# Sparse-attention scores of a two-layer decoder trunk: from one fp32 product to three products of split operands

## What is computed

```
q: (512, 8 heads, 128)   k_cmp, k_slc, k_win: per group of 4 heads
kc = compress(k_cmp)                                # 31 keys of 128
p_c = softmax(q @ kc.T * scale + bias)              # masked
p_s = softmax(q @ k_slc.T * scale + bias)           # causal
p_w = softmax(q @ k_win.T * scale + bias)           # causal
o = g0 * (p_c @ v_cmp) + g1 * (p_s @ v_slc) + g2 * (p_w @ v_win)
h = h + concat(y_mla, o * silu(g_nsa), y_mem) @ w_out
```

## Time and profile before

| | |
|---|---|
| median of 3 runs | 2171.14 us (2170.78 to 2171.8) |
| profiled execution | 2172.06 us |
| its span, first to last instruction | 2170.3 us |
| TensorE busy | 2151.5 us (99%) |
| VectorE busy | 1350.6 us (62%) |
| ScalarE busy | 920.8 us (42%) |
| GpSimd busy | 579.5 us (27%) |
| mean granted TensorE clock | 0.999 |

### The profile page before, as it was taken

One profiled execution on the slowest core, in us unless ns is written; L12 is line 12 of the kernel. 1 busy time (PEld: TensorE's weight loads), 2 busy tenths in 40 slices (PEclk: granted clock), 3 DMA queues, 4 the chain that ended last, 5 costly groups with the idle time before them and its releaser, 6 DMA issues. The chain is left out here.

```text
span 2170.3 us, 32485 instructions
## 1 busy us (share of the span) xinstructions
PE 2151.5 (99%) x12292; PEld 1810.8 (83%) x12292; DVE 1350.6 (62%) x2244; ACT 920.8 (42%) x1558; POOL 579.5 (27%) x771
## 2 busy tenths in 40 slices
PE   9999999999999999999999999999999999999998
PEld 8988888888888878888888899899886778788887
DVE  6632456655542237568649778877776648666876
ACT  6432333333332434434444444444433455555443
POOL 2626122223221002112001444444311255221120
PEclk9999999999999999999999999999999999999999
DMA  8645444444445436648644886878747966554674
GB/s 311 205 140 137 125 130 130 118 128 135 137 123 186 128 99 203 222 148 212 175 156 120 203 202 162 202 185 193 176 152 237 293 216 198 173 193 145 226 164 146
DMA packets 222423, 376.19 MB, mean 173 GB/s; under 512 B 22623, under 2 KB 102191, under 8 KB 220099
## 3 DMA queue, kind: packets, MB, share of 16 engines
q1 hardware_dynamic: 125152, 185.36, 27.8%
q0 software_dynamic: 63152, 126.20, 24.2%
q10 hardware_dynamic: 33971, 62.63, 7.9%
HBM read 310.30 MB, written 63.83 MB: 172 GB/s over the span
## 5 line engine op out<-in xcount | busy, mean ns | idle before, releaser
L283 PE MATMUL PS<-A,wsp 128*128 128x512 f32 (+2 forms) x3156 | 693.8, 379 | 2.9 <-issue 1.7
L283 PEld LDWEIGHTS PS<-A,wsp 128*128 128x128 f32 (+1 forms) x3156 | 564.2, 188 | 119.0 <-issue 9.1
L250 DVE TENSOR_TENSOR wsp<-wraw,wsp 128x1024 fp32r<-128x1024 f32 (+1 forms) x295 | 356.5, 1212 | 468.6 <-ACT wsp L243 467.0
L283 PE MATMUL PS<-wsp,A 128*128 128x512 f32 x2352 | 616.2, 403 | 0.0
L243 ACT ACTIVATE wsp<-wraw 128x1024 fp32r<-128x1024 f32 (+1 forms) x295 | 304.9, 1039 | 509.6 <-PE PS L283 406.7
L283 PEld LDWEIGHTS PS<-wsp,A 128*128 128x128 f32 x2352 | 423.8, 189 | 77.5 <-issue 4.8
L2044 PE MATMUL PS<-A,wsp 128*128 128x512 f32 x640 | 222.6, 397 | 0.0
L2046 PE MATMUL PS<-A,wsp 128*128 128x256 f32 x640 | 166.4, 280 | 0.0
L2001 DVE TENSOR_TENSOR wsp<-wraw,wsp 128x1024 fp32r<-128x1024 f32 x80 | 111.3, 1394 | 39.3 <-ACT wsp L1983 39.1
L2044 PEld LDWEIGHTS PS<-A,wsp 128*128 128x128 f32 x640 | 116.2, 188 | 21.8
L2046 PEld LDWEIGHTS PS<-A,wsp 128*128 128x128 f32 x640 | 120.7, 189 | 6.2
(11 more groups left out here) (455 smaller groups left out, 2841.4 us busy)
## 6 DMA issues: line engine op xcount, KB each, us to landing
wraw<-in_even_w_in_dram SPq DMA_DIRECT2D x112, 512.0 KB, 3.7
wraw<-in_odd_w_in_dram SPq DMA_DIRECT2D x96, 512.0 KB, 4.7
wraw<-in_w_out_dram SPq DMA_DIRECT2D x74, 512.0 KB, 4.6
wraw<-in_mem_w_kv_dram SPq DMA_DIRECT2D x32, 512.0 KB, 4.8
wraw<-in_w_out_dram POOLq DMA_DIRECT2D x24, 512.0 KB, 6.5
yO<-stage ACTq DMA_DIRECT2D x12, 1024.0 KB
yE<-stage ACTq DMA_DIRECT2D x10, 1024.0 KB
wraw<-in_odd_w_in_dram POOLq DMA_DIRECT2D x20, 512.0 KB, 8.8
```

The lines of the kernel that those rows point to most:

```text
L250: nc.vector.tensor_tensor(wsp[:, q, 1, :, 0:j["cols"]], wraw[:, q, :, 0:j["cols"]], wsp[:, q, 0, :, 0:j["cols"]].bitcast(F32), ALU.subtrac ...
L283: mm = nc.tensor.matmul(dst, lhs, rhs, start=(s == 0 and kk == 0 and i == 0), stop=(s == j["spc"] - 1 and kk == 1 and i == 2))
```

## The change

The query and key tiles of the sparse heads are now typed float32r. After a load, ScalarE writes a rounded copy of each into a further tile (`act_nsa_high`), and VectorE replaces the loaded tile by itself less that copy (`dve_nsa_low`). A score is three accumulating products: high query by high keys, low query by high keys, high query by low keys. Keys are loaded and split once for a group of four heads, in a buffer for each group, with the loads of head 0 and of head 4; the other heads load a query and a bias only. The bias now goes ahead of the keys.

The splits of head 0 stand ahead of SEQ1 in both queues: behind the latent attention on ScalarE, behind the fills of P and the gate product on VectorE. Those of head h > 0 stand four steps before its first unit, which is unit k = 8 of head h-1: on ScalarE behind exponential 8 of that head, on VectorE behind normalisation 7. Heads 0 and 4 have three operations on each engine (compressed with selected keys, 544 columns; window keys, 512; query, 512), the others one (query). TensorE waits for the splits (rot_low) ahead of a head's first score.

```diff
+        NSA_AHEAD = 4
         def act_seq(act, t):
...
                 if x < len(t.units):
                     seq_exp(act, t, x)
+                if t.l and x + NSA_AHEAD in t.start[1:8]:
+                    act_nsa_high(act, t.start.index(x + NSA_AHEAD))
...
                 if 0 <= x - 1 < len(t.units):
                     seq_norm(dve, t, x - 1)
+                if t.l and x + NSA_AHEAD in t.start[1:8]:
+                    dve_nsa_low(dve, t.start.index(x + NSA_AHEAD))
...
+        def nsa_operands(h):
+
+            keys = [(nsaKcs[h // 4], nsaKcsH[h // 4]), (nsaKw[h // 4], nsaKwH[h // 4])] if h % 4 == 0 else []
+            return keys + [(nsaQ[h % 2], nsaQh[h % 2])]
+
+        def act_nsa_high(act, h):
+
+            act.wait_ge(a_ld[h % 2], SEQ1.ld0[0] + SEQ1.units[SEQ1.start[h]]["ld"])
+            for whole, high_ in nsa_operands(h):
+                nc.scalar.activation(high_, whole.bitcast(F32), ACT.Copy).then_inc(rot_high, 1)
+
+        def dve_nsa_low(dve, h):
+
+            dve.wait_ge(rot_high, nsa_splits(h))
+            for whole, high_ in nsa_operands(h):
+                nc.vector.tensor_tensor(whole, whole.bitcast(F32), high_.bitcast(F32), ALU.subtract).then_inc(rot_low, 1)
...
+            def products(pe, bank, i, key, o, w):
+
+                if i == ORDER[0] and key == 0 and o <= NPAD:
+                    pe.wait_ge(rot_low, nsa_splits(h))
+                low, high_ = (nsaKcs, nsaKw)[key][grp], (nsaKcsH, nsaKwH)[key][grp]
+                rows = slice(i * P, i * P + P)
+                nc.tensor.matmul(bank[:, 0:w], nsaQh[r][:, rows], high_[:, o:o + w], start=True, stop=False)
+                nc.tensor.matmul(bank[:, 0:w], nsaQ[r][:, rows], high_[:, o:o + w], start=False, stop=False)
+                return nc.tensor.matmul(bank[:, 0:w], nsaQh[r][:, rows], low[:, o:o + w], start=False, stop=True)
...
             def load_qk(pool, s_):
-                pool.dma_start(nsaQ[r], yO[1024 + h * P:1152 + h * P, :]).then_inc(s_, 16)
+                pool.dma_start(nsaQ[r].bitcast(F32), yO[1024 + h * P:1152 + h * P, :]).then_inc(s_, 16)
+                pool.dma_start(nsaB[r], biasD[:, h, :]).then_inc(s_, 16)
+                if h % 4:
+                    return
                 for k in range(2):
-                    pool.dma_start((nsaKs, nsaKw)[k][r], yO[2560 + 256 * k + grp * P:2688 + 256 * k + grp * P, :]).then_inc(s_, 16)
-                pool.dma_start(nsaB[r], biasD[:, h, :]).then_inc(s_, 16)
+                    dst = (nsaKcs[grp][:, NPAD:NPAD + 512], nsaKw[grp])[k]
+                    pool.dma_start(dst.bitcast(F32), yO[2560 + 256 * k + grp * P:2688 + 256 * k + grp * P, :]).then_inc(s_, 16)
...
             act_att(act, MLA)
+            act_nsa_high(act, 0)
             act_seq(act, SEQ1)
...
             dve.wait_ge(p_zero, 5)
+            dve_nsa_low(dve, 0)
             dve_seq(dve, SEQ1)
```

More of the change, by code:

```diff
@@ L3425, in build, with nsa_splits @@
         nsaK0 = A[:, 16:20, :].rearrange("p k t -> p (k t)").bitcast(F32)
-        nsaQ, nsaKw = [[nsaK0[:, o:o + 512], S[:, 8192 + o1:8704 + o1]] for o, o1 in ((0, 0), (1024 + NPAD, 512))]
-        nsaKcs = [nsaK0[:, 512:1024 + NPAD], S[:, 10240:10752 + NPAD]]
-        nsaKc, nsaKs = [[k[:, o:o + n] for k in nsaKcs] for o, n in ((0, NPAD), (NPAD, 512))]
+        nsaQ = [A[:, 16, :], S_rounded[:, 8192:8704]]
+        nsaQh = [A[:, 15, :], A[:, 35, :]]
+        nsaK0r = A[:, 17:20, :].rearrange("p k t -> p (k t)")
+        nsaK0h = A[:, 32:35, :].rearrange("p k t -> p (k t)")
+        nsaKcs = [nsaK0r[:, 0:512 + NPAD], S_rounded[:, 10240:10752 + NPAD]]
+        nsaKcsH = [nsaK0h[:, 0:512 + NPAD], S_rounded[:, 15264:15776 + NPAD]]
+        nsaKw = [nsaK0r[:, 512 + NPAD:1024 + NPAD], S_rounded[:, 8704:9216]]
+        nsaKwH = [nsaK0h[:, 512 + NPAD:1024 + NPAD], S_rounded[:, 15776 + NPAD:16288 + NPAD]]
+        ROT_SPLITS = 9
+        def nsa_splits(h):
+            return ROT_SPLITS + h + 1 + 2 * (1 + (h >= 4))
+        def nsa_operands(h):
[9 more added lines that the diff above has]
+                nc.vector.tensor_tensor(whole, whole.bitcast(F32), high_.bitcast(F32), ALU.subtract).then_inc(rot_low, 1)
         nsaB = [a_tiles(36, 3)[:, 0:LB], S[:, 13312:13312 + LB]]
@@ L3435, in nsa_head @@
             r, grp = h % 2, h // 4
-            keys = (nsaKs[r], nsaKw[r], nsaKc[r])
+            def products(pe, bank, i, key, o, w):
[6 more added lines that the diff above has]
+                return nc.tensor.matmul(bank[:, 0:w], nsaQh[r][:, rows], low[:, o:o + w], start=False, stop=True)
@@ L3438, in score @@
             def score(i, which, w):
-                q = nsaQ[r][:, i * P:i * P + P]
                 if i == 3:
-                    return lambda pe, bank: nc.tensor.matmul(bank[:, 0:w], q, keys[which][:, 0:w], start=True, stop=True)
+                    return lambda pe, bank: products(pe, bank, i, which % 2, NPAD if which == 0 else 0, w)
                 if which == 0:
-                    return lambda pe, bank: nc.tensor.matmul(bank[:, 0:NPAD + w], q, nsaKcs[r][:, 0:NPAD + w], start=True, stop=True)
+                    return lambda pe, bank: products(pe, bank, i, 0, 0, NPAD + w)
@@ L3444, in score @@
                 if which == 1:
-                    return lambda pe, bank: nc.tensor.matmul(bank[:, 0:w], q, nsaKw[r][:, 0:w], start=True, stop=True)
+                    return lambda pe, bank: products(pe, bank, i, 1, 0, w)
                 return None
             def load_qk(pool, s_):
-                pool.dma_start(nsaQ[r], yO[1024 + h * P:1152 + h * P, :]).then_inc(s_, 16)
+                pool.dma_start(nsaQ[r].bitcast(F32), yO[1024 + h * P:1152 + h * P, :]).then_inc(s_, 16)
+                pool.dma_start(nsaB[r], biasD[:, h, :]).then_inc(s_, 16)
@@ L3453, in load_qk @@
                 if h == 0:
                     pool.wait_ge(cmp_out, 32)
-                pool.dma_start(nsaKc[r], cmpD[grp, :, 0:NPAD]).then_inc(s_, 16)
+                pool.dma_start(nsaKcs[grp][:, 0:NPAD].bitcast(F32), cmpD[grp, :, 0:NPAD]).then_inc(s_, 16)
             def load_v(pool, s_):
@@ L3472, in nsa_head @@
                                       gate=gtmS[:, i, col:col + 1], first=which == 0, last=which == 2))
-            return head_units(h, units, ld=80 * (h // 2 + 1), vld=48 * (h // 2 + 1), vn=3, out_gate=nsaG[r],
+            return head_units(h, units, ld=32 * (h // 2 + 1) + (0 if r else 48 * (grp + 1)), vld=48 * (h // 2 + 1), vn=3, out_gate=nsaG[r],
                               gate_rows=yO[5120 + h * P:5248 + h * P, :], load_qk=load_qk, load_v=load_v)
-        SEQ1 = Seq(1, [u for h in range(8) for u in nsa_head(h)] + [u for h in range(4) for u in mem_head(1, h, yO, 3584, 6144, 320, 192)], OUT1A, h1D, 1)
+        SEQ1 = Seq(1, [u for h in range(8) for u in nsa_head(h)] + [u for h in range(4) for u in mem_head(1, h, yO, 3584, 6144, (224, 128)[h % 2], 192)], OUT1A, h1D, 1)
         def pe_nsa_gates(pe):
```

## The result

The changed kernel takes 2177.35 us (median of 15 runs, 2175.75 to 2183.75), the kernel before 2171.09 (15 runs): a ratio of 1.0028, 95% interval 1.0022 to 1.0035. It is 6.3 us slower, where 2171.4 was forecast and 2175.8 was the upper end. A second profile of the same kernel (e11) had the fill at 1831.98. That is +4.6 of the +6.3.

What follows compares the result with a forecast made beforehand. TensorE, busy 2151.5 of 2170.3 us, was taken to bound the kernel; −4.0 products, +3.0 start, +1.1 group 1 keys and +0.2 query splits gave +0.3, so 2171.4 us, range 2167.5 to 2175.8.

Steps and rivals of the forecast that it cites:

- products, eight heads: Scores of the sparse heads: three split products cost 4.17 us a head against 4.67, saving 4.0 us over eight heads.
- start of head 0, the gap: Ahead of head 0's first score: TensorE waits for VectorE's subtractions, score 3.25 us late, net cost +3.0 us (2.7 to 3.4).
- rival 4: The 3.3 us gap ahead of head 0 lowers TensorE's clock to 1.2 GHz, adding 3.0 us: 2174.4 us; chance 0.07.
- keys of group 1, head 3: At k=8 of head 3, three high parts delay unit 6's eviction and transpose 7: +1.1 us (0.5 to 2).
- query splits, the others: One query split for each of heads 1 to 3 and 5 to 7, nearly hidden: +0.2 us in sum (0 to 1).
- rival 2: In all scores, a product costs only its columns, with no floor: 9.0 us saved, 2166.4 us; chance 0.04.
- the dear bound of the products: Sparse-head scores at 0.231 us for 512 columns and 0.12 for narrow products: 0.3 us saved a head, 2.4 in all.
- the 0.2% called undetectable: Whole kernel: a change under 0.2% (4.3 us) is about what measurement cannot tell from none.
- covered by the same stall: Head 3, transpose 8: normalisation 8 ends near 1916.9, transpose runs at 1917.2 after transpose 7's stall, so no further cost.
- free, or a tenth now and then: Query splits, judged in head 1: slack of 0.1 and 0.6 us at transposes 7 and 8, so almost no cost.
- rival 3: Query splits in six heads are not hidden, 0.8 us lost in each: +4.8 over forecast, 2176.2 us; chance 0.13.
- Elsewhere the clock stood at 1.00: Outside the kernel's last 8 us, TensorE's granted clock was claimed to stay at 1.00, in shorter gaps.

Runs made afterwards that it cites:

- e11: The changed kernel run and profiled again with no edit: 2176.67 us, ratio 1.0022 to the kernel before.
- e9: The changed kernel with only VectorE's subtractions for heads 1 to 7 one step later, ScalarE's high parts unmoved: 2173.82 us, ratio 1.0011.
- e1: The changed kernel with 13 spare 512-column products keeping TensorE at work in the gap ahead of head 0's first score: 2176.17 us, ratio 1.0024.
- e6: The kernel before with only the loads changed (keys once for a group, bias first), scores still fp32, no splits: 2171.19 us, ratio 0.9999.
- e4: The changed kernel with later heads' splits spread, one ScalarE high part a step and VectorE subtracting one step later: 2172.29 us, ratio 1.0003.
- e5: The kernel before with four more fills of P on VectorE and a TensorE wait for them ahead of the first sparse score: 2175.36 us, ratio 1.0020.
- e7: The changed kernel with splits and waits kept, but each score one fp32 product of the high parts: 2181.15 us, ratio 1.0044.
- e2: The changed kernel with VectorE's three subtractions for head 0 ahead of the four fills of P: 2175.07 us, ratio 1.0019.
- e10: The changed kernel with spread splits, head 0's subtractions ahead of the fills, two weight splits moved into the heads, residual load two steps later: 2168.25 us, ratio 0.9984.
- e8: The changed kernel with spread splits, head 0's subtractions ahead of the fills and two weight splits moved into the heads: 2169.17 us, ratio 0.9987.

## Why the prediction was wrong

The forecast was a sum of −4.0 + 3.0 + 1.1 + 0.2 = +0.3 us. Measured in the section of the change:

| term | forecast | measured | from |
|---|---|---|---|
| products, eight heads | −4.0 | −4.1 | heads 1, 2, 5, 7: 0.51 us each |
| start of head 0, the gap | +3.0 | +3.2 | e9, where the clock stayed up: 26.78 − 24.12 + 0.53 |
| start of head 0, the clock | rival 4 (+3.0) | +1.3 to 1.5 | e1; e9 against the first profile and e11 |
| keys of group 1, head 3 | +1.1 | +2.2 | 1.71 + 0.5 |
| query splits, the others | +0.2 | +1.8 | head 4 0.78 + 0.5, head 6 0.02 + 0.5 |
| sum | +0.3 | +4.5 | profile: +4.58 |

**Right:** the products, in their sum. From the start of a score to the start of the instruction behind it, a head's nine scores take 4.60 us before and 4.08 after (medians over the heads at full clock), so 0.52 is saved where 0.50 was forecast. The single prices were less exact and partly cancel: 512 columns take 0.70 us and not 0.675, the one fp32 product of 32 columns 0.14 and not 0.22, three narrow products 0.25 to 0.30 and not 0.33. That the saving comes out so exactly is luck. Within three narrow products the second and third end 0.11 us after the one before, as in rows 4, so rival 2 fails. The Trainium skill (TensorE: Matmul & The Clock Gate, section on fast weight load) has the fast load on for every type but FP32. But its table gives a gain for fp8 and bf16 and none for fp32, and does not name float32r, so the prediction read more into it than it says; this trace shows no such gain. Also right were the gap's place and size (first score 3.19 us late against 3.25), the third score's delay (3.0 us, in e9), and that the loads buy nothing (e6).

Two slips in the working change nothing: the dear bound of the products adds up to 4.32 us a head, so 2.8 saved and not 2.4; and the 0.2% called undetectable was too wide, since the interval measured here is under 0.1% to either side.

**Wrong, first:** the step "covered by the same stall" for transpose 8 in head 3, and "free, or a tenth now and then" for the query splits. For transpose 8 I followed only normalisation 8, through VectorE's queue. It also needs the eviction of unit 7 (gap of 1.08 us), and that stands in ScalarE's queue behind exponential 9, which waits for maximum 9, the very instruction that I had as 2.7 us late. I named what was queued behind the high parts on ScalarE, but not what was queued there behind an exponential that VectorE holds up. e9 shows both chains apart, e4 removes both. Head 3 cost +2.2 us for +1.1, the query splits +1.8 for +0.2. For these it was rival 3's effect by another link than rival 3 named, in two of six heads and not in all.

**Wrong, second:** the sum had the clock at nothing, and it stood as a rival at 0.07. It falls in most executions: 5 of 6 profiles with this gap have it (after, e4, e5, e7 and e11 do, e9 does not). e5 shows that the gap alone does it. Its price is half of what rival 4 said, 1.3 to 1.5 us for 3 (1.7 in e7), because the clock is low for 3.4 us of time, in which at most 1.7 us of work is lost, and not for 3 us of work. The Trainium skill (TensorE: Matmul & The Clock Gate, HAM oscillation) warns that TensorE waits between bursts throw it back to the half clock. The trace agrees, at a gap of 3.03 us. "Elsewhere the clock stood at 1.00" was true of the profile of the kernel before, but by chance: its gap of 1.49 us at 1626 us had the clock fall in other executions, while e2's 0.72 and 1.15 did not.

**Open:** some 1.7 us of the 6.3 lie outside the section, as far as one profile and a difference of medians can be set against each other. 0.9 of them is the wait for the second memory head's keys (8.01 us from the first to the fifth memory score, 7.11 before). The keys land 7.6 us after their issue, where it was 6.7 before, just in time for the fifth score. The wait goes when the residual load is moved (e10), so that load in flight matters. Why the keys land later in kernels with splits and not in e6, where loads are issued at the same distances, was not found. The rest was not placed. The tail of the changed kernel's first profile has 1.3 us of waits for weights, and those of e1 and e11 have none, so these are not the change's.

## What to carry to other kernels

On a kernel whose TensorE is 99% busy, price a new operation on ScalarE or VectorE by every instruction that stands behind it in both queues: each wait across engines passes the delay into the other queue, and what TensorE needs may stand there behind something that it doesn't need (here an eviction behind an exponential, and in head 4 behind a weight split too). Put one engine's half of a pair a step behind the other's, and one operation in a step; here that turned +6.3 into +1.3 us (e4), and with a start without a gap into −2.6 (e8), or −3.0 with the residual load moved too (e10). A gap of 3.0 to 3.3 us on TensorE cost 4.4 to 4.9 us in five profiles of six, with the low clock behind it.

## What the runs showed of the hardware that was not expected

- A TensorE gap of 3.0 to 3.3 us was followed by a mean granted clock of 0.57 to 0.62 over the next 4 us in five profiles of six, and in one (e9) by 1.00. Idle times of 1.5 to 1.8 and 0.38 us close together were followed by the low clock in six profiles, and in others with as much idle time by none. Gaps of 0.72 and 1.15 us (e2, one profile) did not lower it.
- From the start of a score to the start of the instruction behind it, three float32r products with 128 weights against one fp32 product take 0.70 against 0.86 us at 512 columns, 0.35 against 0.43 at 256, 0.30 against 0.27 at 160, 0.28 against 0.22 at 128 and 0.25 against 0.14 at 32 (after and before). They win from 256 columns up and lose at 160 and below.
- The second memory head's keys (128 KB on the GpSimd queue) landed 6.7 us after issue in before, e5 and e6, and 7.3 to 7.7 in the kernels with splits (after, e1 to e4, e7 to e9, e11), with a 1 MB load issued 1.1 us ahead. With that load 2.5 us behind them (e10) they landed in 4.2.
